# Layer norms of a second block: row sums from the residual sum and squares on ScalarE, in place of VectorE's statistics

## The reference

```
def layer_norm_2(x, g, b):
    mu = mean(x, -1);  var = mean(square(x - mu), -1)
    return (x - mu) * rsqrt(var + 1e-5) * g + b

for i in range(2):                      # layer: retention, then neighbourhood
    h = x * (1 + sc1) + sh1             # per-channel scale and shift
    y, yc = mixer_i(h, hc)
    x = layer_norm_2(ALPHA * x + g1 * y, ln_g[i, 0], ln_b[i, 0])
    h = x * (1 + sc2) + sh2
    x = layer_norm_2(ALPHA * x + g2 * (square(relu(h @ w1[i])) @ w2[i]), ln_g[i, 1], ln_b[i, 1])
    # layer 0 does the same to a second stream of 256 tokens, ctx; layer 1 does not
```

## Time and profile before

| what | value |
|---|---|
| runs | 2146.02, 2144.08, 2140.91 us; median 2144.08 |
| profiled execution | 2141.47 us; its span 2139.7 us |
| TensorE busy | 2072.1 us, 97% of the span |
| VectorE busy | 1295.3 us, 61% |
| ScalarE busy | 866.2 us, 40% |
| GpSimd busy | 223.0 us, 10% |
| granted TensorE clock | 0.996 of full speed over the span |
| chain that ended last | PE 76%, DVE 13%, issue 3%, POOL 3%, ACT 2%, DMA 2% |

### The profile page before, as it was taken

How to read it: one execution, slowest core, us unless ns; L and a number is a source line. 1 busy time by engine, 2 the same in 40 slices (tenths; PEclk the granted TensorE clock), 3 DMA queues, 4 the chain that set the end, 5 groups by cost and what they waited for, 6 DMA issues and landing times.

```text
span 2139.7 us, 31542 instructions
## 1 busy us (share of the span) xinstructions
PE 2072.1 (97%) x12313; PEld 1695.3 (79%) x12313; DVE 1295.3 (61%) x2063; ACT 866.2 (40%) x1435; POOL 223.0 (10%) x231
## 2 busy tenths in 40 slices
PE   8998999999999999999999999999999999999997
PEld 7776899877768998877777778788888787777996
DVE  5656777476567774744434368634445734767667
ACT  5433466344334665422222225322322434645452
POOL 2020200000200000000000004100000430713000
PEclk9999999999999999999999999999999999999999
DMA  8477665644776655422222322333232373425662
GB/s 245 158 255 256 182 177 176 194 121 158 267 248 194 176 177 177 131 60 98 59 98 59 98 60 79 98 99 95 85 99 95 99 133 109 61 56 157 196 185 90
DMA packets 304629, 297.47 MB, mean 139 GB/s; under 512 B 10454, under 2 KB 223778, under 8 KB 304400
## 3 DMA queue, kind: packets, MB, share of 16 engines
q1 hardware_dynamic: 297360, 276.92, 42.2%
q0 software_dynamic: 7168, 19.13, 4.1%
HBM read 294.97 MB, written 1.05 MB: 138 GB/s over the span
## 4 chain that ended last, share of the span: by engine, by line
PE 76%; DVE 13%; issue 3%; POOL 3%; ACT 2%; DMA 2%; DVEq 0%; ACTq 0%; SPq 0%; POOLq 0%
PE ps L431 22%; PE ps L433 21%; PE ps L432 21%; DVE w_lo L420 4%; PE ps L1917 2%; PE ps L499 2%; DMA nb<-in_nat_rpb 1%; POOL nb L2299 1%; POOL nb L2303 1%; DVE hid L1539 1%; PE ps L695 1%; PE ps L703 1%; DVE qkv L1207 1%; PE ps L705 1%; PE ps L1900 1%
## 5 line engine op out<-in xcount | busy, mean ns | idle before, releaser
L420 DVE TENSOR_TENSOR w_lo<-raw,w_hi 128x1024 fp32r<-128x1024 f32 x428 | 525.5, 1270 | 354.7 <-ACT w_hi L412 354.5
L412 ACT ACTIVATE w_hi<-raw 128x1024 fp32r<-128x1024 f32 x428 | 428.9, 1052 | 566.9 <-PE ps L431 467.7
L431 PE MATMUL ps<-zt_hi,w_hi 128*128 128x512 f32 (+1 forms) x816 | 275.1, 337 | 3.8 <-issue 1.4
L432 PE MATMUL ps<-zt_lo,w_hi 128*128 128x512 f32 (+1 forms) x816 | 273.8, 336 | 0.0
L433 PE MATMUL ps<-zt_hi,w_lo 128*128 128x512 f32 (+1 forms) x816 | 273.8, 336 | 0.0
L431 PE MATMUL ps<-xt_hi,w_hi 128*128 128x256 f32 x896 | 256.4, 286 | 10.6 <-DVE w_lo L420 8.6
L432 PE MATMUL ps<-xt_lo,w_hi 128*128 128x256 f32 x896 | 251.9, 281 | 0.0
L433 PE MATMUL ps<-xt_hi,w_lo 128*128 128x256 f32 x896 | 251.8, 281 | 0.0
L431 PEld LDWEIGHTS ps<-xt_hi,w_hi 128*128 128x128 f32 x896 | 169.5, 189 | 19.6 <-DVE w_lo L420 10.2
L431 PEld LDWEIGHTS ps<-zt_hi,w_hi 128*128 128x128 f32 x816 | 153.5, 188 | 24.7 <-issue 2.8
L433 PEld LDWEIGHTS ps<-xt_hi,w_lo 128*128 128x128 f32 x896 | 169.5, 189 | 0.0
(11 more groups left out here) (379 smaller groups left out, 3519.8 us busy)
## 6 DMA issues: line engine op xcount, KB each, us to landing
raw<-in_mlp_w SPq DMA_DIRECT2D x128, 512.0 KB, 4.5
raw<-in_ada_w SPq DMA_DIRECT2D x96, 512.0 KB, 5.2
raw<-in_w_up SPq DMA_DIRECT2D x88, 512.0 KB, 5.0
raw<-in_w_in SPq DMA_DIRECT2D x56, 512.0 KB, 4.7
raw<-in_ret_w_in SPq DMA_DIRECT2D x48, 512.0 KB, 4.3
raw<-in_w_down SPq DMA_DIRECT2D x44, 512.0 KB, 4.3
raw<-in_nat_w_in SPq DMA_DIRECT2D x24, 512.0 KB, 5.1
raw<-in_w_out SPq DMA_DIRECT2D x16, 512.0 KB, 4.7
```

Source lines behind the costliest of these rows:

```text
L412: nc.scalar.activation(w_hi[:, t, w], raw[:, s, w], ACT.Copy).then_inc(on("w_hi"), act.gives("w_hi"))
L420: ins = nc.vector.tensor_tensor(w_lo[:, t, w], raw[:, s, w], w_hi[:, t, w].bitcast(F32), ALU.subtract)
L431: first = nc.tensor.matmul(out_ap, l_hi, r_hi, start=start, stop=False)
L432: nc.tensor.matmul(out_ap, l_hi, r_lo, start=False, stop=False)
```

## The change

The second block's four norms get mean and variance in another way; everything else stays. `bn_stats`, `bn_aggr` and the addition of 1e-5 leave VectorE. The residual sum becomes a `scalar_tensor_tensor` in every case (by 1.0 where x was scaled ahead), with a row sum as a second output (`accum_out`), which doesn't need the sum to be waited for in the first half. After a tile's second half one VectorE instruction of one column makes minus the mean. ScalarE then squares x plus that over 1024 columns into `y` (which nobody reads until it is overwritten) with a row sum as a second output (`act_square`). GpSimd divides the row sum by 1024 and adds 1e-5 (a new `tensor_scalar`) and raises to -0.5 as before. The two places that subtracted the mean now add its negative.

```diff
-            if form == "ahead":
-                V.tensor_tensor(x, x, yt, ALU.add).then_inc(on("v_step"), dve.gives("v_step"))
-            else:
-                V.scalar_tensor_tensor(x, x, ALPHA, yt, ALU.mult, ALU.add).then_inc(
-                    on("v_step"), dve.gives("v_step"))
-            dve.eng.wait_ge(on("v_step"), dve.given("v_step"))
-            o = 32 * (t % 2) + 6 * c
-            V.bn_stats(small[:, o:o + 6], x).then_inc(on("v_step"), dve.gives("v_step"))
+            o = 32 * (t % 2)
+            V.scalar_tensor_tensor(x, x, 1.0 if form == "ahead" else ALPHA, yt, ALU.mult, ALU.add,
+                                   accum_out=small[:, o + c:o + c + 1]).then_inc(on("v_step"), dve.gives("v_step"))
             if c == 1:
-                o = 32 * (t % 2)
                 dve.eng.wait_ge(on("v_step"), dve.given("v_step"))
-                V.bn_aggr(small[:, o + 12:o + 14], small[:, o:o + 12]).then_inc(on("v_step"), dve.gives("v_step"))
-                dve.eng.wait_ge(on("v_step"), dve.given("v_step"))
-                V.tensor_scalar(small[:, o + 16:o + 17], small[:, o + 13:o + 14], LN_EPS, None, ALU.add).then_inc(
-                    on("pow_in"), dve.gives("pow_in"))
+                V.tensor_scalar(small[:, o + 12:o + 13], small[:, o:o + 1], small[:, o + 1:o + 2], -1.0 / D,
+                                ALU.add, ALU.mult).then_inc(on("mean"), dve.gives("mean"))
...
+        def act_square(act, t):
+
+            o = 32 * (t % 2)
+            act.eng.wait_ge(on("mean"), act.takes("mean"))
+            A.activation(y[:, t, :], x_of(t), ACT.Square, bias=small[:, o + 12:o + 13],
+                         accum_out=small[:, o + 16:o + 17]).then_inc(on("ssq"), act.gives("ssq"))
+
         def act_norm4(act, coefs):
+            act_square(act, 0)
+            act_square(act, 1)
             for t in ALL:
                 act_turned(act, t, (t, 4 + t), coefs[stream_of(t)])
+                if t < 2:
+                    act_square(act, 2 + t)
                 if t in (1, 3):
                     split_hi(act)
...
         def pool_powers(pool, tiles):
             for t in tiles:
-                pool.eng.wait_ge(on("pow_in"), pool.takes("pow_in"))
+                pool.eng.wait_ge(on("ssq"), pool.takes("ssq"))
                 c = 32 * (t % 2) + 16
+                G.tensor_scalar(small[:, c:c + 1], small[:, c:c + 1], 1.0 / D, LN_EPS, ALU.mult, ALU.add).then_inc(
+                    on("p_step"), pool.gives("p_step"))
+                pool.eng.wait_ge(on("p_step"), pool.given("p_step"))
...
-            for _ in range(4):
+            for _ in range(3):
                 split_hi(act)
+            for t in LAT:
+                act_square(act, t)
+            split_hi(act)
             for n, t in enumerate(LAT):
                 act_turned(act, t, (4 + 2 * n, 5 + 2 * n), 6)
...
             act_mlp(act, LAT)
+            for t in LAT:
+                act_square(act, t)
```

More of the change, by code:

```diff
@@ L1712, in dve_normal @@
             V.tensor_scalar(y[:, t, :], x_of(t), small[:, o + 12:o + 13], small[:, o + 16:o + 17],
-                            ALU.subtract, ALU.mult).then_inc(on("zn"), dve.gives("zn"))
+                            ALU.add, ALU.mult).then_inc(on("zn"), dve.gives("zn"))
         def open_hh(dve):
@@ L2261, in dve_final @@
                 V.scalar_tensor_tensor(y[:, t, :], x_of(t), small[:, o + 12:o + 13], gn2[:, 0, :],
-                                       ALU.subtract, ALU.mult).then_inc(on("v_step"), dve.gives("v_step"))
+                                       ALU.add, ALU.mult).then_inc(on("v_step"), dve.gives("v_step"))
                 dve.eng.wait_ge(on("v_step"), dve.given("v_step"))
```

## The result

| what | before | after |
|---|---|---|
| median of 20 runs each, us | 2143.38 (2140.74 to 2146.02) | 2147.60 (2144.19 to 2151.00) |
| profiled execution, its span | 2141.47, 2139.7 | 2147.56, 2145.8 |
| VectorE busy | 1295.3 | 1280.8 |
| ScalarE busy | 866.2 | 880.0 |
| GpSimd busy | 223.0 | 223.5 |

The ratio after to before is 1.0018, 95% interval 1.0011 to 1.0025: 3.9 us slower, between 2.4 and 5.4. The prediction said +4.5 and 2148.6. The change of load is as planned, 14.5 us off VectorE and 13.8 onto ScalarE, and the kernel got slower all the same.

What follows compares the result with a forecast made beforehand. TensorE, busy 97%, was taken as the main bound, with the norms' waits set by VectorE, ScalarE and GpSimd. 2.65 + 3.4 - 1.15 - 0.4 = +4.5 us on 2144.08 gave 2148.6; range 2142.4 to 2153.5.

Steps and rivals of the forecast that it cites:

- line of 4.3 us: Whole kernel: 0.2%, 4.3 us, is about what measuring can tell from no change; it divides same from faster or slower.
- Row sum free: VectorE's residual sum with a row sum costs 0.69 us as before, plus 0.08 for who needs the sum.
- Rival C: VectorE's row sum halves the rate, +0.59 us per residual sum; total +8.8 us, 2152.9; chance 0.12.
- Squares at 1.13, result at 1.22: On ScalarE each square of 1024 columns holds the queue 1.13 us, its row sum ready at 1.22.
- Norm 1, +2.65: Norm 1: ScalarE's squares make its weight split, and GpSimd's stream behind, 2.65 us late; costs 2.65 us.
- Norm 2, +3.4: Norm 2: ScalarE's split 3.8 us late, less 0.4 of slack at the second unit's remainder; costs 3.4 us.
- Rival B: Behind norm 2 the split isn't late enough to matter; total +2.3 us, 2146.4; chance 0.15.
- GpSimd pair at 1.20: With VectorE idle, GpSimd's two one-column instructions per tile take 0.56 us each, 1.20 with their wait.
- Norm 3, -1.15: Norm 3: turned tile 2 starts at 1935.8 instead of 1936.97, power and transposes done by 1935.6; gains 1.15 us.
- Norm 4, -0.4: Norm 4: the last tile's pass begins at 2133.65 instead of 2134.05; gains 0.4 us.
- Rival D: In all four norms VectorE's relief decides, ScalarE taking each square at once; total -1.7 us, 2142.4; chance 0.20.
- Rival E: More than the forecast, by small GpSimd instructions near 1.5 us or longer TensorE pauses lowering its clock; 2151 and up; chance 0.05.

Runs made afterwards that it cites:

- early: New method in norms 1 and 2 only, norms 3 and 4 with VectorE's statistics as in the kernel before; ratio to the kernel before 1.0028.
- fill: Changed kernel with two more filler matmuls around tile 3's transposes in norms 1 and 2; ratio to the kernel before 1.0018.
- Tiles01: Changed kernel, but in norms 1 and 2 tiles 2 and 3 have VectorE's statistics again; ratio to the kernel before 0.9997.
- short: Changed kernel, but squares of tiles 2 and 3 in norms 1 and 2 cover only 128 columns; ratio to the kernel before 1.0010.
- keep3: Changed kernel with four instead of five groups of filler matmuls ahead of norm 3's transposes; ratio to the kernel before 1.0028.
- go: Changed kernel with GpSimd's stream behind norm 2 held until the first of the VectorE split's two instructions; ratio to the kernel before 1.0015.
- best: Kernel before with new norms 3 and 4, norm 3's fourth ScalarE split behind the turned tiles, three filler groups for five; ratio 0.9990.
- late: Changed kernel, but norms 1 and 2 have VectorE's statistics again; ratio to the kernel before 0.9997.

## Why the prediction was right

Most of it held, step by step. Of the 1.0 us between the 2148.6 forecast and the 2147.60 measured, 0.7 is the starting point: the median of the kernel before was 2144.08 over three runs and is 2143.38 over twenty. By the line of 4.3 us that the chances use, +3.9 counts as no change (given 0.46) and the forecast's own +4.5 as slower (0.47).

- **Row sum free.** Held: 0.69, a reader of 0.08. Rival C is out. The Trainium skill (Vector Engine (DVE) Microarchitecture Reference, Points that are easy to get wrong) says that two non-bf16 SBUF sources halve the throughput of this form, with no read port left for the accumulator. The row sum shows no such price here: 128x512 float32 take 692 ns with it and 692 without. Whether the plain form is itself a slow one is not settled by that. It costs as much as `bn_stats` with one source, which is what the prediction went by, but over 1024 columns it takes 1.28, where a `tensor_scalar` with one SBUF tensor takes 0.81.
- **Squares at 1.13, result at 1.22.** 1.15, and the reader ends 1.24 behind the start.
- **Norm 1, +2.65.** +2.62. The middle step, TensorE's start, was 0.4 too late, and the end right, because the end hangs on ScalarE's split, late by 2.61 where 2.65 stood.
- **Norm 2, +3.4.** Split late by 3.37 where 3.8 stood; slack 0.2 to 0.3 where 0.4 stood; +3.04 (early) to +3.18 (after). The 0.4 was a misreading: at 1699.11 begins a piece of the chain, while the matmul itself, the second unit's first, begins at 1698.95, 0.28 behind the remainder. The mechanism, the remainder of the second unit between ScalarE and GpSimd, is shown by early and fill. Rival B said the split might not be late enough: out. The sign that was named against B, TensorE idle for 2 to 3.4 us ahead of the second unit, is missing in the changed kernel's own trace, because of the slow clock; early (2.49) and fill (2.48) have it.
- **GpSimd pair at 1.20.** Wrong size: 0.19 and 0.55, 0.83 with the wait between. I took the new one-column `tensor_scalar` to cost what the power costs. Twice 0.37 is most of what tile 3 and the product came too late in the forecast, 1.2 against 0.40.
- **Norm 3, -1.15.** -0.73. The step that failed is "the power and the transposes are done by 1935.6": they weren't, since the fillers ahead of the transposes, 4.54 us of TensorE's own queue, had not been counted. Turned tile 2 began 5.47 behind the product, not within the 5 us that the prediction named as its sign. With four groups of fillers for five the stretch is 1.28 shorter than before.
- **Norm 4, -0.4.** -0.48.
- **Rival D**, that VectorE's relief decides, is out for norms 1 and 2: it needed ScalarE free for each square at once and gave each of them about nothing, and they lose 2.6 and 3.0 to 3.2, with ScalarE's queue late by 2.61 and 3.37. Tiles01 adds that 8 of 24 statistics can leave VectorE there and move nothing. In norms 3 and 4 the relief does decide.
- **Rival E's clock.** The counts above speak for it, without proving that the longer pauses bring the fall about, and the sum has no term for it. In the changed kernel's trace the fall hid in the wait, and the time stayed far from E's 2151; in early, short and keep3 it came in the second unit and cost 1.7 on top.

The sum of 4.5 against 4.59 by stretches owes something to luck: norm 2 was 0.2 to 0.4 too dear and norm 3's gain 0.4 too large, and the fall of the clock that the sum left out landed, in the trace compared, where it cost next to nothing.

## What to carry to other kernels

Work that is moved to an idler engine costs nothing only where that engine's queue is empty: for each moved instruction ask what stands behind it in the new queue and whether its input is there when its turn comes. Here the squares of tiles 0 and 1 were free and those of tiles 2 and 3 cost 5.7 us. And when a trace shows a slow clock just where a wait was expected, cut several traces at the same instructions before naming either: the one can hide in the other. Let the cuts go on a unit or two behind the wait, too, since a slow clock may follow it.

## What the runs showed of the hardware

- At the product behind norm 1 or 2 the granted clock fell to half (0.50) for some 3 to 7 us in 4 of 13 traces (after, go, best, late), after TensorE's short pauses (1.46 and 1.18 us in best, 0.74 and 1.22 in late); other executions with the same pauses had no fall there. It costs up to 2.9 us at such a place.
- In three more traces (early, short, keep3) it fell for 3.4 us about 1 us behind a wait of 2.06 to 2.49 for a weight remainder, and the unit of 10.99 took 12.7. Fill has the same wait of 2.48, more filler matmuls ahead, and no fall.
- A one-column GpSimd `tensor_scalar` takes 0.19 us where VectorE is idle, up to 0.39 beside it; the power 0.55 and up to 1.60 beside a pass of VectorE over two SBUF tensors that began first. Begun 0.01 ahead of such an instruction (1673.99 in after) it took 0.55.
- VectorE's one-column `tensor_scalar` that makes the mean, with a second operand from SBUF, takes 0.21, the form with constants 0.15.
